# The modulation's products in the slots of the sparse attention, with the weights as the stationary operand

## The reference

```python
sh1, sc1, g1, sh2, sc2, g2 = jnp.split(
    (jax.nn.silu(c) @ ada_w[layer] + ada_b[layer])[:, None, :], ADA_CHUNKS, axis=-1)
csh1, csc1, cg1, csh2, csc2, cg2 = jnp.split(
    jax.nn.silu(c_ctx) @ ada_w[layer] + ada_b[layer], ADA_CHUNKS, axis=-1)
...
h = modulate(rmsnorm_2(x, norm1_g[layer]), sh1, sc1)
```

## Time and profile before

| what | value |
|---|---|
| median of 3 runs (lowest, highest) | 3683.35 us (3675.93, 3684.28) |
| profiled execution, its span | 3693.07 us, 3691.6 us |
| mean granted clock of PE | 0.944 of 2.4 GHz |
| PE, PEld busy | 3388.8 us (92%), 2798.5 us (76%) |
| DVE, ACT, POOL busy | 2330.3 us (63%), 1228.1 us (33%), 748.8 us (20%) |
| DMA over the span | 515.15 MB, mean 140 GB/s |

### The profile page before, as it was taken

One profiled execution on the slowest core, in us unless ns is written; L12 is line 12 of the kernel. 1 busy time (PEld: TensorE's weight loads), 2 busy tenths in 40 slices (PEclk: granted clock), 3 DMA queues, 4 the chain that ended last, 5 costly groups with the idle time before them and its releaser, 6 DMA issues. The chain is left out here.

```text
span 3691.6 us, 44814 instructions
## 1 busy us (share of the span) xinstructions
PE 3388.8 (92%) x17156; PEld 2798.5 (76%) x17156; DVE 2330.3 (63%) x4524; ACT 1228.1 (33%) x2087; POOL 748.8 (20%) x703
## 2 busy tenths in 40 slices
PE   7999899999999999997988989678899999999778
PEld 5555446888866688885776868668899999999777
DVE  4773334646455565454553348998968878878776
ACT  2343223323323332233452223223433333333333
POOL 1001222000100030004000010106834444444331
PEclk9678999999999999998998989789999999999989
DMA  3002332223211122222111222324588888888773
GB/s 131 12 7 89 119 125 66 97 95 102 89 51 46 41 97 94 100 92 67 57 40 63 97 69 86 135 99 180 210 285 298 310 299 294 315 291 301 255 267 112
DMA packets 181765, 515.15 MB, mean 140 GB/s; under 512 B 14769, under 2 KB 75185, under 8 KB 174897
## 3 DMA queue, kind: packets, MB, share of 16 engines
q1 hardware_dynamic: 127840, 305.69, 24.9%
q0 software_dynamic: 40464, 160.45, 12.0%
q10 hardware_dynamic: 13248, 46.15, 3.2%
HBM read 477.10 MB, written 35.13 MB: 139 GB/s over the span
## 5 line engine op out<-in xcount | busy, mean ns | idle before, releaser
L222 PE MATMUL bank<-h_hi,w_hi 128*128 128x512 f32 (+1 forms) x2720 | 1045.4, 384 | 95.7 <-ACT w_hi L197 20.1
L222 PE MATMUL bank<-h_lo,w_hi 128*128 128x512 f32 (+1 forms) x2720 | 1027.2, 378 | 0.0
L203 DVE TENSOR_TENSOR w_lo<-w_raw,w_hi 128x1024 fp32r<-128x1024 f32 (+1 forms) x508 | 647.2, 1274 | 282.1 <-ACT w_hi L197 280.7
L197 ACT ACTIVATE w_hi<-w_raw 128x1024 fp32r<-128x1024 f32 (+1 forms) x508 | 545.0, 1074 | 524.4 <-PE bank L222 461.2
L222 PE MATMUL bank<-h_hi,w_lo 128*128 128x512 f32 (+1 forms) x2720 | 647.6, 376 | 30.4 <-DVE w_lo L203 29.8
L222 PEld LDWEIGHTS bank<-h_hi,w_hi 128*128 128x128 f32 x2720 | 529.6, 195 | 183.7 <-issue 46.9
L222 PEld LDWEIGHTS bank<-h_hi,w_lo 128*128 128x128 f32 x2720 | 501.7, 193 | 102.9 <-DVE w_lo L203 36.7
L222 PEld LDWEIGHTS bank<-h_lo,w_hi 128*128 128x128 f32 x2720 | 531.4, 195 | 63.6 <-issue 7.7
L222 PE MATMUL bank<-e_hi,w_hi 128*128 128x384 f32 x832 | 285.9, 344 | 35.0 <-DVE x L2258 25.3
L2101 POOL DMA_INDIRECT own_row<-in_u_rows,own_e x128 | 198.2, 1548 | 440.2 <-DVE own_g L1999 180.7
L222 PE MATMUL bank<-e_lo,w_hi 128*128 128x384 f32 x832 | 282.6, 340 | 0.0
(11 more groups left out here) (400 smaller groups left out, 4614.4 us busy)
## 6 DMA issues: line engine op xcount, KB each, us to landing
w_raw<-in_w SPq DMA_DIRECT2D x476, 512.0 KB
ada_w<-in_ada_w POOLq DMA_DIRECT2D x24, 1024.0 KB, 5.1
expert_weights<-G ACTq DMA_DIRECT2D x24, 1024.0 KB, 4.2
Gin<-expert_weights SPq DMA_DIRECT2D x16, 1536.0 KB, 14.8
w_raw<-in_w SPq DMA_DIRECT2D x32, 704.0 KB
hidden_ahead<-u_stage ACTq DMA_DIRECT2D x40, 192.0 KB, 1.8
ahead<-hidden_ahead SPq DMA_DIRECT2D x10, 768.0 KB, 6.8
na_bias<-in_bias ACTq DMA_DIRECT2D x4, 896.0 KB, 4.6
```

What stands on the lines that cost most here:

```text
L197: sc.activation(w_hi[s][:, 0:n], w_raw[raw_slot[u]][:, 0:n], ACT.Copy).then_inc(*w_hi_made.next(u))
L203: ve.tensor_tensor(w_lo[s][:, 0:n], w_raw[raw_slot[u]][:, 0:n], w_hi[s][:, 0:n], ALU.subtract).then_inc(*w_lo_made.next(u))
L222: m = te.matmul(out, wt, moving, start=(not low and k == 0 and moving is hi), stop=(low and k == len(blocks) - 1))
```

## The change

The 24 steps leave the stick-breaking stage with their copies, turning products, additions, transfers and the Silu on ACT. In the sparse attention each slot from 3 to 47 gets one step and slot 2 gets three, 48 steps in all. Such a step takes half of a weight buffer: 8 products in which a 128 x 128 block of ada_w is stationary and silu(c), 128 x 2, moves. The result comes out with features on partitions, two columns per step, in the bank that held the pair's query projection, and needs no turning. It is issued behind the transposes and ahead of the query's pieces. After every twelfth slot DVE adds the bias for 12 steps at once, and that addition now is the bank's last reader. The silu is a sigmoid on ACT beside that of the gates and a product on DVE, during the projections. POOL issues the 24 transfers of 1 MB, from the end of the projections on, since the buffers lie where tiles of the projections lay; transfer k waits for step 2k-3. The three scalings (scaled_g) of the modulated norms move from the end of the one stage to the end of the other.

```diff
@@ nsa @@
+        silu = sb(st, "silu_c", [P, KT, 2])
+        ada_in = [loaded(f"ada_in{b}") for b in range(2)]
...
+        ada_w = [sb(st, f"ada_w{b}", [P, KT, 256]) for b in range(2)]
...
+            sc.activation(silu[:, :, :], col("c", 0, 16).rearrange("p (k c) -> p k c", c=2), ACT.Sigmoid).then_inc(*act.next("sigmoid c"))
...
+            ve.wait_ge(*act.at("sigmoid c"))
+            ve.tensor_tensor(silu[:, :, :], silu[:, :, :], col("c", 0, 16).rearrange("p (k c) -> p k c", c=2), ALU.mult).then_inc(*dve.next("silu"))
...
+        def ada_tensor(g):
+            k, half = divmod(g, 2)
+            if half == 0:
+                te.wait_ge(*ada_in[k % 2].at(k))
+            if g == 0:
+                te.wait_ge(*dve.at("silu"))
+            for c in range(KT):
+                m = te.matmul(lin[UQ[g // 12] % 2][:, g % 12 * 2:g % 12 * 2 + 2], ada_w[k % 2][:, c, half * P:(half + 1) * P], silu[:, c, :],
+                              start=(c == 0), stop=(c == KT - 1))
+            m.then_inc(*pe.next("ada", g))
+
+        def ada_vector(p):
+            ve.wait_ge(*pe.at("ada", 12 * p + 11))
+            bias = col("ada_b", 12 * p, 12).unsqueeze(2).to_broadcast([P, 12, 2])
+            ve.tensor_tensor(mod[:, 12 * p:12 * p + 12, :], lin[UQ[p] % 2][:, 0:24].rearrange("p (n c) -> p n c", c=2), bias,
+                             ALU.add).then_inc(*dve.next("mod", p))
+            bank_of.taken(UQ[p], dve)
...
+                for n in range(3) if g == 2 else (g,) if 2 < g < slots else ():
+                    ada_tensor(n)
                 if g < slots and p < 3:
                     run(query, 1)
...
+                if g % 12 == 11:
+                    ada_vector(g // 12)
...
+        def gpsimd():
+            after(gp, "nsa projections")
+            for k in range(N_ADA // 2):
+                if k >= 2:
+                    gp.wait_ge(*pe.at("ada", 2 * k - 3))
+                gp.dma_start(ada_w[k % 2][:, :, :], io["ada_w"][k]).then_inc(*ada_in[k % 2].next(k))
@@ stick @@
-        def ada_sums(k):
-            te.wait_ge(*ada_in[k % 2].at(k))
...
-            for c in range(KT):
-                m = te.matmul(x_bank[0:2, 0:256], silu[:, c, :], ada_w[k % 2][:, c, :], start=(c == 0), stop=(c == KT - 1))
-            m.then_inc(*pe.next("ada", k))
-
-        def ada_turn(k):
-            te.wait_ge(*dve.at("ada rows", k))
-            for n in range(2):
-                m = te.matmul(x_bank[:, 256 + 2 * n:258 + 2 * n], rows_of[:, n * P:(n + 1) * P], ident[0:2, 0:2], start=True, stop=True)
-            m.then_inc(*pe.next("ada turned", k))
...
                 run(more, 4)
-                if m < steps:
-                    for a in range(6 * p + (n * 3) // 2, 6 * p + ((n + 1) * 3) // 2):
-                        ada_sums(a)
-                        ada_turn(a)
                 run(more, 2)
...
-            sc.preload_act_table_set("silu_and_others")
-            sc.activation(silu[:, :, :], col("c", 0, 16).rearrange("p (k c) -> p k c", c=2), ACT.Silu).then_inc(*act.next("silu"))
...
-                    for a in range(6 * p + (n * 3) // 2, 6 * p + ((n + 1) * 3) // 2):
-                        ada_rows(a)
-                        ada_add(a)
...
-                if m < steps:
-                    while fetched < min(ADA_STEPS, 2 + 6 * p + ((n + 1) * 3) // 2):
-                        ada_fetch(fetched)
-                        fetched += 1
```

More of the change, by code:

```diff
@@ L32 @@
 N_ADA = 6 * KT
-ADA_STEPS = N_ADA // 2
 HK = 128
@@ L874, in vector @@
                     ve.tensor_tensor(o_lo[:, 4 + p2, :], o_banks[p2 % 2][:, :], o_hi[:, 4 + p2, :], ALU.subtract).then_inc(*dve.next("nsa out", p2))
+            ve.wait_ge(*dve.here())
+            for s in range(3):
+                chunk, c, name = ((1, 0, "norm1"), (1, 1, "norm1"), (4, 0, "norm2"))[s]
+                ve.scalar_tensor_tensor(scaled_g[:, s, :], mod[:, chunk * KT:(chunk + 1) * KT, c], 1.0, col(name, 0, KT), ALU.add, ALU.mult).then_inc(*dve.next("scaled_g"))
+        def gpsimd():
[4 more added lines that the diff above has]
+                gp.dma_start(ada_w[k % 2][:, :, :], io["ada_w"][k]).then_inc(*ada_in[k % 2].next(k))
         first_tensor()
@@ L882, in nsa @@
         vector()
+        gpsimd()
         ended("nsa")
@@ L933, in stick @@
         rest = [sb(st, f"sb_later{hh}", [P, T]) for hh in range(2)]
[L934 to L937, removed]
         steps = 4 * TT
@@ L1091, in vector @@
                     ve.tensor_tensor(o_lo[:, p2, :], o_bank[:, :], o_hi[:, p2, :], ALU.subtract).then_inc(*dve.next("sb out", p2))
[L1092 to L1095, removed]
         def gpsimd():
             after(gp, before)
[L1100 to L1107, removed]
             gp.wait_ge(*strict_in.at("in"))
```

## The result

The changed kernel takes 3768.97 us (median of 4 runs, 3768.08 to 3790.08) against 3682.67 for the kernel before (4 runs, 3675.93 to 3684.28): a ratio of 1.025 (1.021 to 1.029), 86 us slower. Its profiled execution took 3768.15 us with a span of 3766.7.

The account below looks back on a forecast made before the run. PE was taken to bound both stages, with its granted clock mattering as much. Sparse attention +184 and stick-breaking −98 gave +86 us on the 3683 us median: 3769 us, ends 3732 to 3802 (chance 0.69); the overall range was 3686 to 3812.

Parts of the forecast that it names:

- The price of a step: Sparse attention: each added step of 16 passes costs PE 1.62 us at the high level, 3.42 us at the low.
- Rival C: Sparse attention: a pass costs 0.101 us at either clock level; −37 us in all, 3646 us; chance 0.02.
- The clock: Sparse attention: narrow steps act as pauses, most slots lose the high level; granted clock falls from 0.70 to near 0.55.
- Rivals A: Sparse attention: the clock keeps its present pattern; +13 us in all, 3696 us; chance 0.15.
- Rival B: Sparse attention: added passes close gaps in PE's queue, 2.4 GHz throughout; −88 us in all, 3595 us; chance 0.09.
- The sparse attention's sum: Sparse attention: 164 us of low-level steps plus 52 for slowed slots, less 17 and 15: 184 us longer (159 to 199).
- the high moments that are left: Sparse attention: high clock returning briefly near runs of 16 passes saves 15 us (0 to 40).
- the 17 us of cover: Sparse attention: PE's present waiting hides 17 us of the steps, from 8 (exponential waits) and 10 (slow sums).
- The stick-breaking stage's sum: Stick-breaking stage: removed steps free 121.5 us of PE's queue, less 10, 4 and 9: 98 us saved (85 to 110).
- The 14 us that were to stay in PE's queue: Stick-breaking stage: time not recovered because steps covered chain waits, 10 us in the last pair, 4 in the first three.
- The small terms: Both stages: silu, additions, bank wait and weight transfers taken as 0, with 5 us kept in the range.
- rival D: Sparse attention: weights arrive late and PE waits in most slots; 2 us lacking per transfer brings 3817 us; chance 0.05.

Follow-up runs that it names:

- the 128-column form: Changed kernel with silu repeated 64 times, so 128 columns move per step product instead of 2; 3609.34 us, ratio to the kernel before 0.979.
- the fill: Changed kernel with 128 moving columns, plus eight unused products in each slot of the stick-breaking stage's last pair; 3604.39 us, ratio to the kernel before 0.978.

## Why the prediction was right

**The price of a step** was right within 0.15 us. The rows that gave 1.62 and 3.42 us were those of the norms, with one column. After the change a step at each level reads:

```profile
109.48 3.41 PE L775 MATMUL bank<-silu_c,ada_w 128*128 128x2 f32 x16
112.75 0.77 PE L221 MATMUL bank<-h_lo,w_hi 128*128 128x512 f32 x1
...
301.55 1.84 PE L775 MATMUL bank<-silu_c,ada_w 128*128 128x2 f32 x16
303.25 0.58 PE L221 MATMUL bank<-h_hi,w_hi 128*128 128x512 f32 x1
```

From a step's start to the next operation's that is 112.75 − 109.48 = 3.27 us low and 303.25 − 301.55 = 1.70 high, for 3.42 and 1.62 foreseen. Rival C, a pass that costs the same at either level, is out. By the Trainium skill ("TensorE: Matmul & The Clock Gate", "LDWEIGHTS (loading the stationary operand)") a load takes its columns over 1.2 in ns, 107 for 128, with no term for the clock: the high step fits (1.70 / 16 = 0.106 us), the low one doesn't (3.27 / 16 = 0.204), and the measurement decides.

**The clock** was the step on which all hung, and it was right: 0.55 foreseen, 0.55 found. Rivals A (0.70) and B (1.00) fell on the same number. The row that bore it was the one of the norms' passes, 0.50 in them and behind them, and it was thin: those 12 passes last 2.7 us and follow eight others behind a wait,

```profile
1703.00 1.38 PE L447 MATMUL bank<-ones,acc 128*128 128x1 f32 x8 [4.29 <-POOL norm_v L1244]
```

so it left open whether the wait or the narrow passes kept the clock low, and what a longer run of them would do. That the reading came out as it did is in part luck. The experiments turned it from an argument into a cause (0.55, 0.60, 0.84, 0.98 with 2, 32, 64 and 128 columns, nothing else changed), and slot 2 of after has 10.26 us of narrow passes at 0.50. Rival B is nearly what the 128-column form does. The rule behind it in the Trainium skill (same page, "Part 1: The HAM clock gate"), that activity releases the throttle, agrees with that form (0.98); after, where PE is counted busy for 390.45 of 393.10 us and the clock is 0.55, shows that being counted busy did not release it here. Slices 2 to 4 of the page, said to be at 6 to 7 tenths, read 6, 7 and 8; nothing hangs on it.

**The sparse attention's sum** was 184 us and came out at 174.5. The term that was off is that of the high moments that are left. I took 15 us for them. A clock of 0.55 is 0.05 / 0.50 × 393.1 = 39 us at the high level, some 5 of them behind the last scores; the other 34 would have taken 34 × 1.67 = 57 us at the low level, so 23 are saved. That is 8 of the 9.5 us. Two more terms were off and pull against each other. The low steps cost 3.27 to 3.34 us for 3.42, a few us less in all. And the 17 us of cover were too many: of the 8 in 16 waits for the exponential the trace of before has 4.3 in ten waits, and PE's whole idle time in the stage went from 218.60 − 212.06 = 6.5 to 2.7 us. The 10 us that were taken in slow passes no row keeps apart.

**The stick-breaking stage's sum** was −98 and came out at −95.6. PE now waits for GpSimd, 9.4 us in six waits for 1.8 in one before, all in the last pair; the timeline of after, with the idle time before it in brackets:

```profile
629.99 0.85 PE L1018 MATMUL bank<-sb_ls,sb_v 128*64 128x128 f32 x4 [1.69 <-POOL sb_ls L1112]
...
639.48 2.07 PE L999 MATMUL bank<-sb_q,sb_k 64*128 64x512 f32 x2
...
652.50 2.08 PE L1005 MATMUL bank<-sb_lk,tri 128*128 128x512 f32 x2 [1.32 <-POOL sb_lk L1116]
```

And the low clock in those slots, taken at 9 us (0 to 20), is worth 10.8 by the fill: slot 15 takes 652.50 − 639.48 = 13.0 us here, and 8.8 with the clock held, which is the length that the sum had for it. The 14 us that were to stay in PE's queue were not measured by themselves.

**The small terms** were nothing, as taken. PE waited for the weights once, 0.2 us (the rows of the page after), and GpSimd waited 333.1 us in 22 waits for PE to be done with a buffer, so rival D is out. DVE's additions waited 1.0 us in three waits. The wait of GpSimd for the buffers' tiles at the end of the projections cost PE nothing that shows.

**The total** agrees better than its parts: +86 by the sum, +86.3 by the medians, but +75.1 between the two profiled spans (+174.5 − 95.6 − 3.8), because before's profiled execution lies 10 us above its median. The parts' errors and that offset happen to cancel; a few us of the agreement are chance.

## What to carry to other kernels

Before a product is turned so that its weights are stationary and only a column or two move, count what the form does to PE's clock and not only its passes: look in the trace for a run of such passes and read the granted clock in and behind it. Where the form is wanted (no turning, the result on the right partitions), repeat the moving operand through a zero step and leave the further columns unread: here 128 columns turned a loss of 86 us into a gain of 77, while 32 columns still lost 1.4%. To compare two forms of a stage, multiply its length by its granted clock: where the products agree, the difference is most likely the clock's. (The product scales waits for other engines too, which don't go with PE's clock, so small differences in it say nothing.)

## What the runs showed of the hardware that was not expected

- More columns cost next to nothing, up to 128. At the high level a step is 1.70 us from its start to a unit's pass with 2 columns (301.55 to 303.25) and with 128 (205.63 to 207.33), and 1.77 and 1.88 us ahead of weighted sums (279.05 to 280.82, 201.65 to 203.53). Both forms load the same weights, which would explain the equal pace.
- The same stage with the same instructions has different clocks in different executions: the sparse attention of before, of the kernel with the turned steps in the other stage, and of its 128-column form, which issue the same work there, ran at 0.70, 0.70 and 0.73, in 218.6, 218.7 and 212.3 us; without the steps it had 0.66 and 228.4 us. Each is one profiled execution. The runs of one kernel scatter as well: over 19 us with 64 columns, 21 without the steps, 22 in after (one run of the four), but 5 with 128 columns; and the time goes with the mean clock (before: 3678.80 us at 0.949, 3691.04 at 0.943). So 6 to 10 us between two profiles of such a stage are no effect of an edit by themselves. Why the level differs stays open.
- PE's waits in the last pair cost twice: the wait, and the low level for the products behind it. Eight products of no use in each of the last pair's four slots, 1.95 us a time, made the stage 10.8 us shorter.
